# Second block of a two-block transformer kernel: next weights split before a convolution's SiLU, head norms before a split, retention's token tiles and last value load in another order

## The reference, cut to what matters

```python
h = rmsnorm(x, g[0])
proj = h @ w_in[l]
(mq, mk, mv, mo, mi, mf, dq, dk, dv, rq, rk, rv, rg, gates) = split_in(proj)
qk = jax.nn.silu(causal_dwconv(jnp.concatenate([mq, mk], axis=-1), mlstm_conv[l]))
hm = mlstm(q, k, v, i, f)                  # 4 heads of 256
hm = jax.nn.sigmoid(mo) * head_rms(hm)
hd = diff_attention(dq, dk, dv, lam)       # 8 heads
hr = retention(rq, rk, rv)                 # 4 heads of 256
hr = jax.nn.silu(rg) * head_rms(hr)
y = gm * (hm @ w_mlstm_out) + gd * (hd @ w_diff_out) + gr * (hr @ w_ret_out)
```

## Time and profile before

| | before |
|---|---|
| median of 3 runs | 2353.7 us (2353.33 to 2354.11) |
| profiled execution, first to last instruction (span) | 2350.7 us |
| PE busy | 2312.0 us, 98% |
| DVE busy | 1547.4 us, 66% |
| ACT busy | 1003.1 us, 43% |
| mean granted TensorE clock | 0.997 of full speed |
| projection, first product to the last group's end | about 1103 to 1391 us |
| mLSTM heads | about 1396 to 1526 us |
| retention heads | about 1570 to 1665 us |

### The profile page before, as it was taken

One profiled execution on the slowest core, in us unless ns is written; L12 is line 12 of the kernel. 1 busy time (PEld: TensorE's weight loads), 2 busy tenths in 40 slices (PEclk: granted clock), 3 DMA queues, 4 the chain that ended last, 5 costly groups with the idle time before them and its releaser, 6 DMA issues.

```text
span 2350.7 us, 28530 instructions
## 1 busy us (share of the span) xinstructions
PE 2312.0 (98%) x11228; PEld 1910.6 (81%) x11228; DVE 1547.4 (66%) x2296; ACT 1003.1 (43%) x1729; POOL 115.2 (5%) x204
## 2 busy tenths in 40 slices
PE   8999999999999999999999999999999999999998
PEld 7778888888888888888777887887777888888887
DVE  4767876866777887768888876533467545474655
ACT  4444443434544344435445555512246535333323
POOL 3000000000000000000101111101100000000000
PEclk9999999999999999999999999999999999999999
DMA  4123423333213323322655662333432132323232
GB/s 145 47 82 119 132 90 130 104 108 108 73 37 108 108 72 125 108 90 90 171 188 160 215 197 92 128 122 108 145 82 66 55 108 90 103 78 121 75 125 72
DMA packets 180445, 257.04 MB, mean 109 GB/s; under 512 B 10671, under 2 KB 115340, under 8 KB 180064
## 3 DMA queue, kind: packets, MB, share of 16 engines
q1 hardware_dynamic: 164704, 204.82, 27.1%
q0 software_dynamic: 15616, 50.52, 7.2%
HBM read 238.50 MB, written 19.96 MB: 110 GB/s over the span
## 4 chain that ended last, share of the span: by engine, by line
PE 89%; DVE 7%; ACT 2%; issue 1%; DMA 1%; POOL 0%; SPq 0%; DVEq 0%; ACTq 0%
PE B L702 46%; PE A L702 32%; PE C L702 8%; DVE WL L2284 1%; DVE WL L2292 1%; PE C L1164 1%; DVE RAW L2959 0%; DVE ar L2492 0%; PE C L1458 0%; ACT WH L1596 0%; PE C L1306 0%; DMA X<-in_x 0%; DVE Y L2614 0%; DMA projected<-Y 0%; DVE st L2595 0%
## 5 line engine op out<-in xcount | busy, mean ns | idle before, releaser
L702 PE MATMUL B<-XH,WH 128*128 128x512 f32 (+1 forms) x1432 | 542.4, 383 | 1.4 <-ACT XH L1653 0.8
L702 PE MATMUL B<-XH,WL 128*128 128x512 f32 (+1 forms) x1432 | 535.1, 378 | 0.0
L702 PE MATMUL B<-XL,WH 128*128 128x512 f32 (+1 forms) x1432 | 520.4, 379 | 3.0 <-DVE XL L2440 2.8
L2284 DVE TENSOR_TENSOR WL<-RAW,WH 128x1024 fp32r<-128x1024 f32 (+3 forms) x318 | 362.7, 1182 | 220.7 <-ACT WH L1596 220.2
L1596 ACT ACTIVATE WH<-RAW 128x1024 fp32r<-128x1024 f32 (+3 forms) x334 | 324.8, 1022 | 324.1 <-PE A L702 176.9
L702 PEld LDWEIGHTS B<-XH,WH 128*128 128x128 f32 x1432 | 269.3, 188 | 61.5 <-issue 7.6
L702 PEld LDWEIGHTS B<-XH,WL 128*128 128x128 f32 x1432 | 269.2, 188 | 50.5
L702 PEld LDWEIGHTS B<-XL,WH 128*128 128x128 f32 x1432 | 260.4, 189 | 52.5 <-DVE XL L2440 4.6
L702 PE MATMUL A<-WH,YH 128*128 128x512 f32 x728 | 284.7, 391 | 0.9 <-DVE WL L2292 0.6
L702 PE MATMUL A<-WH,YL 128*128 128x512 f32 x728 | 283.5, 389 | 0.0
L702 PE MATMUL A<-WL,YH 128*128 128x512 f32 x728 | 283.3, 389 | 0.0
(11 more groups left out here) (408 smaller groups left out, 3512.9 us busy)
## 6 DMA issues: line engine op xcount, KB each, us to landing
RAW<-in_w_in SPq DMA_DIRECT2D x42, 1024.0 KB, 5.3
RAW<-in_mlp_w_up SPq DMA_DIRECT2D x32, 1024.0 KB, 5.4
RAW<-in_mlp_w_down SPq DMA_DIRECT2D x26, 1024.0 KB, 5.3
RAW<-in_w_ffn_in SPq DMA_DIRECT2D x22, 1024.0 KB, 5.1
projected<-Y POOLq DMA_DIRECT2D x28, 512.0 KB, 5.1
ar<-projected POOLq DMA_DIRECT2D x16, 512.0 KB, 4.3
RAW<-in_w_in SPq DMA_DIRECT2D x16, 512.0 KB, 4.7
RAW<-in_w_ffn_out SPq DMA_DIRECT2D x8, 1024.0 KB, 5.1
```

What stands on the lines that cost most here:

```text
L702: return nc.tensor.matmul(dst, l, r, start=first, stop=last)
L2284: x = tt(WL[s][:, part], RAW[s][:, part], f32(WH[s][:, part]), ALU.subtract)
```

## The change

There are four edits, and no instruction is added or removed.

1. In the projection, ACT does `split(d + 7)` before the convolution's SiLU, and DVE moves `with_fourth(g)` from before the convolution to behind `project_weights(g + 1)`.
2. In mLSTM, ACT's `head_rms` and DVE's `denominators` and `values_by_token` come before `split(QK_AT[query] + 1)`.
3. In retention's first three heads, the token tiles are taken in the order 2, 3, 0, 1 by PE, ACT, POOL and DVE.
4. There, POOL issues the next head's `load_values` after the inverse roots of two tiles instead of four, behind a wait for PE's last values.

```diff
+def tiles_of(name, i):
+    return (2, 3, 0, 1) if name == "ret" and i < 3 else range(T)
...
         def decayed_values(name, i, rounds, at, v, width):
             pe.wait_ge(s_("lv_in"), 16 * (nth(name, i) + 1))
-            for t in range(T):
+            for t in tiles_of(name, i):
...
             functioned(g, 1)
+            split(d + 7)
             if g < 4:
                 after_conv(0, g // 2, (g % 2,))
-            split(d + 7)
...
         def head_rms(name, i, inv):
-            for t in range(T):
+            for x, t in enumerate(tiles_of(name, i)):
...
-                    act.wait_ge(s_("head_o"), T * nth(name, i) + t + 1)
+                    act.wait_ge(s_("head_o"), T * nth(name, i) + x + 1)
...
             head_part(*key[:2], 1)
+            head_rms("ml", i, True)
             split(QK_AT[query] + 1)
-            head_rms("ml", i, True)
...
             low_both(d + 6, XP_THIRD)
-            with_fourth(g)
             if g < 4:
                 convolution(0, g // 2, g % 2)
...
             if g + 1 < len(XP):
                 project_weights(g + 1)
+            with_fourth(g)
...
             head_part(*key[:2], 1)
-            split(QK_AT[query] + 1)
             denominators(i)
             values_by_token("ml", i)
+            split(QK_AT[query] + 1)
...
-        def head_rms(name, i):
-            for t in range(T):
-                pool.wait_ge(s_("head_ss"), T * nth(name, i) + t + 1)
+        def head_rms(name, i, values=None):
+            for x, t in enumerate(tiles_of(name, i)):
+                if values is not None and x == 2:
+                    pool.wait_ge(s_("head_o"), T * nth(name, i) + T)
+                    load_values("rv", values)
+                pool.wait_ge(s_("head_ss"), T * nth(name, i) + x + 1)
...
-            head_rms("ret", i)
+            head_rms("ret", i, i + 1 if i < 3 else None)
             if i < 3:
-                load_values("rv", i + 1)
```

More of the change, by code:

```diff
@@ L2877, in values_by_token @@
         def values_by_token(name, i):
-            for t in range(T):
-                dve.wait_ge(s_("head_r"), T * nth(name, i) + t + 1)
-                if t == 0:
+            for x, t in enumerate(tiles_of(name, i)):
+                dve.wait_ge(s_("head_r"), T * nth(name, i) + x + 1)
+                if x == 0:
                     dve.wait_ge(s_("lo_in"), 16 * (nth(name, i) + 1))
```

## The result

The changed kernel takes 2339.4 us (median of 4 runs, 2338.6 to 2340.3) against 2353.6 us for the kernel before (4 runs, 2353.3 to 2354.1). The ratio is 0.9942 [0.9931, 0.9954]: 14.2 us faster, within 0.5 us of the forecast 2338.9. The profiled execution after spans 2338.5 us, 12.2 less than the profiled one before.

A forecast was written before the change was run, and what follows sets the result against it. TensorE, busy 98%, was taken to bound the kernel, so only its waits and slow clock count. Projection 8.8, mLSTM 3.6 and retention 2.4 sum to 14.8 us: 2353.7 - 14.8 = 2338.9, range 2334 to 2345.

The forecast's parts named there:

- The group ends: Projection: TensorE runs 3.50 us after the weights land; first products still wait 0.2, 0.5, 0.5 and nothing, 1.2 in all.
- Second and third products: Projection: new waits of 0.45 us each for late low parts; 0.95 with slower first issues, at three ends, 2.85.
- Groups 5 to 7 at no net cost: Projection: fifth group waits 0.3 us, sixth 0.5 more, the last end gains 0.8; net nothing.
- The half clock goes with the gaps: Projection: two stretches at half clock, 2 x 1.6 = 3.2 us, are caused by the 2.1 us gaps and go with them.
- mLSTM: Three heads: the 0.9 us wait for the norm and 0.3 of slower issue go, 1.2 by head, 3.6 in all.
- Retention: Edits 3 and 4: 0.3 us in each of two heads, 1.8 up to the last values, together 2.4.
- TensorE starts at 1654.2 + 4.0: Retention's last values: load issued about 1.8 us earlier, used 4.0 after issue as before, so TensorE starts at 1658.2.
- a low clock after a short wait: Sign named beforehand: the prediction is wrong if the low clock shows after a short wait.
- the rival in which the slow clock comes back at another short wait: Rival: the slow clock stays or comes back at another short wait, 3.2 us more, 2342.1; chance 14%.
- DVE keeps up: Rival, projection: the 1.2 and 2.85 us of waits at the group ends don't come, 2334.9; chance 15%.
- The other rivals: Small waits pile up, 2344.9 us, 12%; the split doesn't get ahead, 2347.7, 5%; slower by later landings, 2359.5, 4%.
- The step from span to median: Whole kernel: medians stand 3.0 us above the 2350.7 span and lose the same 14.8, from 2353.7 to 2338.9.

The follow-up runs named there:

- r9: The changed kernel, unaltered, measured again on the chip of r6 to r8: 2340.5 us, ratio 0.9952, against 2352.9 for the kernel before.
- r6: The changed kernel with DVE's `with_fourth` between the convolution and `split(d + 7)`, in DVE's idle time: 2333.5 us, ratio 0.9920.
- r1: Edit 1 alone (projection group ends), edits 2 to 4 undone from the changed kernel: 2343.3 us, ratio 0.9958.
- r4: The changed kernel without edit 4, the value load issued after four inverse roots again: 2340.1 us, ratio 0.9948.
- r10: The changed kernel with ACT's SiLU back ahead of `split(d + 7)`, only DVE's move of edit 1 left: 2342.3 us, ratio 0.9955.
- r2: Edit 2 alone (mLSTM norms ahead of the split), projection and retention as in the kernel before: 2349.8 us, ratio 0.9990.
- r3: Edits 3 and 4 alone (retention's tile order and early value load), the rest as in the kernel before: 2353.5 us, ratio 1.0000.
- r5: The changed kernel with DVE's `with_fourth` back ahead of the convolution, only ACT's move of edit 1 left: 2339.0 us, ratio 0.9942.
- r8: The changed kernel with r6 and r7 together and retention's tiles in the order 0, 2, 1, 3: 2332.7 us, ratio 0.9920.
- r7: The changed kernel with SP's last 1 MB load of retention output weights held until the values have landed: 2337.6 us, ratio 0.9934.

## Why the prediction was right, point by point

**The group ends: right.** The copy starts at the landing, TensorE 3.5 later; the first products waited 0.13, 0, 0.4 and 0 where 0.2, 0.5, 0.5 and 0 stood. The second number differs since these hang on landings, 8.1, 7.5, 8.4 and 6.1 us at the four ends here. In r9, with 8.5, 8.8 and 7.6 at the first three, TensorE shows waits of 0.35, 0.65 and none.

**Second and third products: right in kind, a little too dear.** The waits for L2297 are there. Four products at the second, third and fourth group's start take 22.80, 22.29 and 22.76 instead of 21.76: 1.04, 0.53 and 1.0, together 2.6 against 2.85. That these waits would come was sound; that DVE could do the takings in the idle time that the same edit opened was not seen, and it was worth more than the whole term (r6).

**Groups 5 to 7 at no net cost: nearly.** Without the gap's 1.75, they lost 2.25 us to such waits before (118.24 less 114.24 less 1.75) and lose 2.63 now: 0.4 dearer. The three parts: the fifth group loses 0.5 (0.3 forecast), the sixth 0.6 (0.5), the last end gives 0.8 (0.8).

**The half clock goes with the gaps: right, on the evidence there is.** The kernels without the gaps of 2.1 (after, r1, r4 to r10: nine traces) have full clock from 1100 to 1400 throughout. Of the twelve gaps in before, r2 and r3, five are followed by it. So the gap brings it, but not each time; what tells the one from the other stays open. The waits that it follows in these traces are 1.94 to 2.14 us long.

A wait that no edit touches says the same. Ahead of the projection, at about 1069, TensorE waits 2.13 or 2.14 us for DVE in all twelve traces. In the changed kernel's trace it ends here, and the second row is the clock 2 us later:

```profile
1068.69 1.52 PE L707 MATMUL B<-XL,WH 128*128 128x256 f32 x8 [2.13 <-DVE XL L2445]
```

```profile
1071.00:1072.00 1.00, 1.00 (x7) 1.00 (x6) 1.00 (x2) 0.00 (x0) 0.00 (x0) 0.50 0.00 0
```

The clock falls to 0.50 behind it in six traces (before, after, r3, r5, r8, r10) and stays full in the other six. From that wait's end to the first product of the projection it takes 34.2 to 34.5 us in the first six and 33.1 in the others. A half clock thus costs 1.1 to 1.4 there, and whether an execution has it is part of why executions of one kernel differ. The forecast counted both half clocks of one trace as if each execution had them. With 5 in 12 gaps, four gaps would have 1.7 on average, 2.7 us instead of 3.2: an estimate from few traces.

The rule weighed against this term, from the Trainium skill, "TensorE: Matmul & The Clock Gate", section "Why this matters for your kernels", has the clock drop only after longer idle than that. The traces don't agree with it: 0.50 stands behind waits of 1.94 to 2.14 us, and behind the gaps of 2.1 alone in the projection. A term for it stood rightly in the sum.

**mLSTM: right.** The norm took 6.6 us from the convolution's end to the last value (forecast 6.7) and left 3.0 to spare (2.8). The gain by head is 1.11, from 17.23 to 16.12, against 1.2; the term was read off the fourth head, whose stretch is 16.04.

**Retention: the step that failed.** Two of its three parts hold: the first two heads give 0.25 each (0.3 forecast), the third head's values lead to the scores in 4.31 instead of 5.00, 0.7 (0.77 forecast), and the load is issued 5.1 us behind the start of the third head's values instead of 7.0, 1.8 earlier, as forecast. What failed is "TensorE starts at 1654.2 + 4.0": the 4.0 was kept for a load that had moved into another transfer. Before, SP's 1 MB went out 3.2 us ahead of it, now 1.4, and the landing took 5.6. From the third head's values to the next ones the gain is 0.26 where 1.8 was forecast, and TensorE waits 1.94 instead of 0.4. Behind it the half clock takes some 1.7 more when it comes (96.4 in r5 with it, 94.7 in r10 without, at waits of 2.08 and 2.07). Together that is the term's error of 3.2 us, and more than the whole error in the traces, 14.8 against 12.2; the other terms made up 0.6. r7 takes the other transfer away and gets the forecast 2.4 and a little more.

The forecast had named a low clock after a short wait as a sign of being wrong, and this is one: the rival in which the slow clock comes back at another short wait came true here, at 1.7 us instead of the 3.2 it was given. *DVE keeps up* came true for single waits only (none at two of the four ends). The other rivals didn't come.

**The step from span to median** was the lucky one. The forecast took 3.0 us as fixed between span and median. After, the profiled execution's device time is 2340.3, 1.8 over its span, and the median 0.9 over it. If the same 1.8 lies over the span of before, its profiled execution was about 1 us faster than its median, while that of after was 0.9 slower. Repeated on another chip the gain is 12.4 us (r9, 2352.9 to 2340.5), nearer to the traces' 12.2. That the number came out within 0.5 us owes some 2 us to this.

## What to carry to other kernels

When a wait for a chain of engines is taken out, look at where the reordered engine now idles and put the moved work there, not at the list's next free place: here the same two instructions cost 5 us more behind the split than ahead of it. Two moves that each cut the same chain don't add up, so try each alone. And a load issued earlier is not a load landed earlier: look at what the other queues send in the same microseconds, and move the transfer that has time.

## What the runs showed of the hardware

- A load's landing hangs on its neighbours in time. In the last retention head 512 KB on POOL's queue landed in 3.8 to 4.0 us with no such load ahead of it or 3 us behind a 1 MB load of SP, and in 5.2 to 5.7 when issued 1.4 us behind it. The two value loads ahead of that one, issued 1.5 us behind a 1 MB load, landed in 4.9 to 6.7.
- The landing of one and the same 1 MB load varies by 2 us between executions (6.5, 8.1, 8.2 and 8.5 us at the first group's end in r7, after, before and r9). Waits of 0.2 to 0.8 at the group ends follow it.
- The half clock, 0.50 of full speed, for some 3 us, came behind waits of TensorE of 1.94 to 2.14 us, at the same place in some traces and not in others: behind 5 of the 12 gaps of 2.1 in before, r2 and r3, behind 6 of the 12 waits of 2.13 or 2.14 at 1069, and behind 3 of the 5 waits of 1.94 to 2.08 for the last values (after, r3 and r5, not r4 and r10). Behind 1.67 and 1.59 (r9, r6) it did not come. It costs 1.1 to 1.7 us of a stretch where TensorE has no wait behind it. In r2 a stretch with one was no shorter than with two.
